# The second block's MLP residual turned by VectorE and sixteen transfers instead of by TensorE

## What is computed

```python
def second_block(x, ...):
    ...
    h = h + y @ w_out[l]
    u = _rmsnorm(h, mlp_norm_g[l])
    h = h + jnp.square(jax.nn.relu(u @ w_up[l])) @ w_down[l]   # the MLP and its residual
    h = _rmsnorm(h, final_norm_g)
    return h[:, N_META:]
```

## Time and profile before

| what | value |
|---|---|
| median of 3 runs | 989.25 us (988.41 to 989.67) |
| the profiled execution | 988.87 us |
| its span in the profile | 987.0 us |
| TensorE busy, of the span | 976.6 us, 99% |
| VectorE, ScalarE, GpSimd busy | 627.5, 470.6, 524.9 us |
| HBM traffic | 110.91 MB read, 2.10 MB written |

### The profile page before, as it was taken

The page is one execution under the profiler, slowest core; times in us unless marked ns, Lnnn a source line. Parts: engine busy times, 40 slices in busy tenths (PEclk is TensorE's granted clock), DMA queues, the critical chain, the costliest instruction groups (busy, mean ns, idle before and its releaser), DMA issues.

```text
span 987.0 us, 12665 instructions
## 1 busy us (share of the span) xinstructions
PE 976.6 (99%) x4827; PEld 827.5 (84%) x4827; DVE 627.5 (64%) x938; ACT 470.6 (48%) x746; POOL 524.9 (53%) x625
## 2 busy tenths in 40 slices
PE   9999999999999999999999999999999999999996
PEld 7888888888888888888899988888888888888885
DVE  5782257665373763274669999874962771595696
ACT  4554445554673223442334866554643443353464
POOL 4555555556555895555656778555056037018212
PEclk9999999999999999999999999999999999999998
DMA  7323221212353225623223123468558347536346
GB/s 238 102 78 126 85 87 44 85 41 68 107 175 124 86 86 134 146 87 127 65 86 107 46 74 118 125 237 193 149 175 197 107 147 185 149 87 182 53 85 171
DMA packets 109116, 117.49 MB, mean 119 GB/s; under 512 B 20434, under 2 KB 86512, under 8 KB 109056
## 3 DMA queue, kind: packets, MB, share of 16 engines
q1 hardware_dynamic: 102304, 102.20, 33.1%
q0 software_dynamic: 6448, 14.16, 8.4%
q10 hardware_dynamic: 304, 0.33, 0.1%
HBM read 110.91 MB, written 2.10 MB: 114 GB/s over the span
## 4 chain that ended last, share of the span: by engine, by line
PE 99%; DVE 0%; ACT 0%; DVEq 0%; issue 0%; ACTq 0%
PE ps L585 70%; PE ps L967 15%; PE ps L604 4%; PE ps L730 1%; PE ps L654 1%; PE ps L751 1%; PE ps L715 1%; PE ps L714 1%; PE ps L845 1%; PE ps L1013 1%; PE ps L792 1%; PE ps L637 0%; PE ps L630 0%; PE ps L941 0%; PE ps L879 0%; DVE X L2472 0%
## 5 line engine op out<-in xcount | busy, mean ns | idle before, releaser
L2523 POOL TENSOR_TENSOR wlo<-raw,whi 128x256 fp32r<-128x256 f32 x496 | 400.4, 860 | 216.6 <-ACT whi L1021 216.5
L585 PE MATMUL ps<-Hh,whi 128*128 128x512 f32 x512 | 201.6, 394 | 0.0
L585 PE MATMUL ps<-Hl,whi 128*128 128x512 f32 x512 | 199.5, 390 | 0.0
L1021 ACT ACTIVATE whi<-raw 128x1024 fp32r<-128x1024 f32 (+1 forms) x126 | 132.2, 1050 | 87.4 <-PE ps L585 51.4
L585 PE MATMUL ps<-Ah,whi 128*128 128x512 f32 (+1 forms) x496 | 164.3, 357 | 0.0
L585 PE MATMUL ps<-Al,whi 128*128 128x512 f32 (+1 forms) x496 | 163.5, 356 | 0.0
L585 PE MATMUL ps<-Hh,wlo 128*128 128x512 f32 x512 | 129.4, 389 | 0.0
L585 PEld LDWEIGHTS ps<-Hh,wlo 128*128 128x128 f32 x512 | 96.1, 188 | 20.0
L585 PEld LDWEIGHTS ps<-Hh,whi 128*128 128x128 f32 x512 | 96.2, 188 | 19.6 <-DVE Hl L1620 0.2
L585 PEld LDWEIGHTS ps<-Hl,whi 128*128 128x128 f32 x512 | 96.2, 188 | 19.2
L585 PE MATMUL ps<-Ah,wlo 128*128 128x512 f32 (+1 forms) x496 | 104.8, 356 | 0.0
(11 more groups left out here) (371 smaller groups left out, 1662.8 us busy)
## 6 DMA issues: line engine op xcount, KB each, us to landing
raw<-in_w_in SPq DMA_DIRECT2D x29, 1024.0 KB, 5.3
raw<-in_w_up SPq DMA_DIRECT2D x16, 1024.0 KB, 5.6
Fm<-in_w_down SPq DMA_DIRECT2D x8, 1024.0 KB, 5.0
w_w<-in_w_down POOLq DMA_DIRECT2D x16, 512.0 KB, 5.7
raw<-in_w_in SPq DMA_DIRECT2D x14, 512.0 KB, 3.8
raw<-in_w_att_out SPq DMA_DIRECT2D x4, 1024.0 KB, 5.2
raw<-in_w_sg_out SPq DMA_DIRECT2D x4, 1024.0 KB, 5.2
raw<-in_w_o SPq DMA_DIRECT2D x4, 1024.0 KB, 5.1
```

What stands on the lines that cost most here:

```text
L585: mm = e.matmul(ps[:, bk, 0:c1 - c0], of(j)[:, k % kk, 128 * g:128 * g + 128], x[:, k, c0:c1], start=(start and n == 0), stop=(stop and n ...
L1021: return e.activation(out, src, ACT.Copy, scale=scale)
L2523: ins = e.tensor_tensor(w_lo(j)[:, *cut], raw_tile(j)[:, *cut], f(w_hi(j))[:, *cut], ALU.subtract)
```

## The change

TensorE's and ScalarE's `residual` go. VectorE gets one instead: after `act(0, 3)` it turns x1 in blocks of 32 x 32, two instructions for each `F3[:, n]`, sixteen in all, from `F3` into `F4f`. A 32 x 32 turn leaves each block on the group of 32 partitions on which it was, so SyncE then issues sixteen transfers from SBUF to SBUF: each takes one of four groups of 32 partitions (c) and one of four token groups (i) and copies it, 32 partitions x 32 pieces x 32 floats, to the 32 partitions on which those tokens belong in `Y`. They stand between the two weight blocks that SyncE loads for part 1. The signal `residual_turned` (wait of the first two casts) becomes `residual_blocks`, and VectorE's wait in `out` goes from `residual_set` to `residual_in` of the last transfer; since `out` in part 0 writes `acc`, which is `F4f`, all of part 0's `out` calls now wait for it.

```diff
+        Y_pieces = F1f.rearrange("p (x c f) -> p x c f", c=4, f=32)
+        turned = F4f.rearrange("p (i x f) -> p i x f", i=4, f=32)
@@ sync_program, part loop
                 load_block(up)
+                if part == 1:
+                    w.wait_ge("residual_blocks", 7)
+                    for c in range(4):
+                        for i in range(4):
+                            e.dma_start(Y_pieces[32 * i:32 * i + 32, :, c], turned[32 * c:32 * c + 32, i]).then_inc(
+                                *b.done("residual_in", (c, i), 16))
                 load_block(up + 1)
@@ tensor_program
-            def residual(n):
-                bk = 7 - n % 2
-                ...
-                for i in range(4):
-                    mm = e.transpose(ps[:, bk, 128 * i:128 * i + 128], F3[:, n, 128 * i:128 * i + 128], ident[:])
-                mm.then_inc(*b.done("residual_turned", n))
@@ down_free
                 if n == P_4:
-                    return "residual_set", 7 - r
+                    return "mlp_mean", 0
@@ scalar_program
-            def residual(n):
-                w.wait_ge("x1_late", 3)
-                w.wait_ge("residual_turned", n)
-                src = ps[:, 7 - n % 2, :].rearrange("p (r t c) -> p r t c", r=2, t=2)
-                copy(Y[:, :, n // 4, :, 128 * (n % 4):128 * (n % 4) + 128], src).then_inc(*b.done("residual_set", n))
@@ vector_program
+            def residual(n):
+                to = F4f.rearrange("p (i r c t m f) -> p r c t i m f", i=4, r=2, c=2, t=2, m=4)
+                of = F3[:, n].rearrange("p (r t i f) -> p r t i f", r=2, t=2, i=4)
+                w.wait_ge("products", (J_UP - 1, 3))
+                for r in range(2):
+                    signal = b.done("residual_blocks", n) if r else step()
+                    e.transpose(to[:, r, n // 4, :, :, n % 4], of[:, r]).then_inc(*signal)
@@ out
                     if n != P12 and part == 0:
+                        w.wait_ge("residual_in", (3, 3))
                         e.tensor_copy(y, bank).then_inc(*signal)
                     else:
-                        w.wait_ge(*(("down_out", (part - 1, n, r)) if part else ("residual_set", 7)))
+                        w.wait_ge(*(("down_out", (part - 1, n, r)) if part else ("residual_in", (3, 3))))
@@ part loop of vector_program
                     if n == 3:
+                        if part == 0:
+                            for m in range(8):
+                                residual(m)
                         x_sums(part, P_7)
```

More of the change, by code:

```diff
@@ L994, in tensor_program @@
                         mlp_sums()
-                    if part == 0 and 3 <= n < 7:
-                        residual(2 * n - 6)
-                        residual(2 * n - 5)
                 for n in range(7 if part < 3 else 6):
@@ L1038, in cast @@
                 elif m in (0, 1):
-                    w.wait_ge("residual_turned", 7)
+                    w.wait_ge("residual_blocks", 7)
                 elif before >= 0:
@@ L1529, in scalar_program @@
                     cast(up_tile(0, n) + 2)
-                if n < 7:
-                    residual(2 * n - 6)
-                    residual(2 * n - 5)
                 for i in {3: (0,), 4: (1, 2), 5: (3,), 6: (4,)}.get(n, ()):
```

## The result

The changed kernel takes 992.20 us, median of 8 runs (990.19 to 993.40); the kernel before 988.88 (988.41 to 989.67, 8 runs). The ratio is 1.0032, with a 95% interval of 1.0022 to 1.0041: slower by 0.3%, where I had forecast 985.6 us. The profiled execution took 992.06 us with a span of 990.2, against 988.87 and 987.0.

What follows compares the result with a forecast made beforehand. TensorE, busy 99% of the span at the 2.4 GHz level, bounds the kernel. Removed transposes give -3.63 us, ScalarE, VectorE and SyncE 0: 989.25 - 3.63 = 985.6 us, range 984.8 to 988.6.

Steps and rivals of the forecast that it cites:

- TensorE -3.63: Between up product 3 and the first down product: removing 32 transposes saves 3.63 us, all on the path.
- The 8.7 us of busy time: Summed durations of the 32 transposes, 272 ns each; they overlap, so the prediction did not take this as their price.
- ScalarE and VectorE 0: Dropped copies are off the path; sixteen turns, 5.4 us, fit in VectorE's 12.89 us of idle time: 0 us.
- the lead of VectorE: VectorE takes product 7 out of PSUM by 692 to 694 instead of 698.41, given as 4.4 to 6.7 us earlier.
- SyncE 0: Loads queued behind the sixteen transfers go out later, second block at about 692; needed some 40 us later: 0 us.
- T: Landing of the last of the sixteen transfers, which VectorE's first `out` awaits: 696 us, range 693 to 699.
- The bound of 701.3: Latest landing of the sixteen transfers before TensorE waits, from the 0.56 us slack at P_6's second weight tile.
- P_6's second low part: Tightest place for TensorE: VectorE made this weight tile's part at 720.96, TensorE used it at 721.52, 0.56 us later.
- The price of waiting: At the first `out`: a landing later than 701.3 makes TensorE wait by just the excess.
- Rival 1: Sixteen transfers land late, delaying the first `out`; at twice the piece time +6.1 us, 995.3 us. Chance 0.13.
- Rival 2: GpSimd, held by its own slowed accumulating transfers, delays up tile 7's low part by 0.8 to 3.8 us. Chance 0.13.

Runs made afterwards that it cites:

- The hold: Changed kernel with SyncE's three w_down loads for part 1 held until the accumulating transfer for P_6's first weight sum landed: 986.73 us, ratio 0.9972; repeated, 986.57 us.
- the pure collision: Kernel without the sixteen transfers, with SyncE's second block and three w_down loads held until the low part of P_5's first weight tile is made: 987.97 us, ratio 0.9989.
- thin neighbours: Changed kernel with three of GpSimd's accumulating transfers that run beside the sixteen cut to 64 of 512 columns: 985.67 us, ratio 0.9966.
- the kernel with the first `out` at 699.78: Changed kernel with SyncE's sixteen transfers ahead of both weight blocks, no loads held back: 991.95 us, ratio 1.0026.
- the filler: Changed kernel with eighteen matmuls of no use, 512 columns each, before P_6 in part 0: 990.79 us, ratio 1.0016.

## Why the prediction was wrong

- **TensorE -3.63.** Right: 3.64 in the trace, 3.83 in the time without transfers. The 8.7 us of busy time would have been the wrong number.
- **ScalarE and VectorE 0.** Right, but for a slip in the text (the lead of VectorE was to be 4.4 to 6.4 us by its own numbers, not 6.7). Sixteen turns took 5.33 us (5.4 forecast) and ended at 677.5 (677.4); `x_sums` ran at 677.48; product 7 was taken out of PSUM at 693.84 (692 to 694 forecast).
- **SyncE 0, the step that failed.** I asked only whether what is queued behind the sixteen transfers is needed late itself. It is. But it moved in time, to 699.8 and later, and there it shares the DMA engines with a transfer that is needed at once. I had SyncE free at about 692 and it was free at 699.7. In the kernel before, these loads were spread over 687.6 to 699 and none of them met P_6's. The hold takes this step away (-5.5 us) and the pure collision makes it by itself (+2.6 us, with a landing of 11.6 us). In the changed kernel it cost so much because T had already used up the slack: 3.7 of the 7.9 us in the table are T's.
- **T, mis-sized.** 696 forecast, range 693 to 699, and 701.87 measured. The piece time was about right (16.5 us with thin neighbours, 17.4 in line 508's rows); the neighbours were counted as two transfers of up to 3 us and were three that added 8. By itself T cost little: with the hold, it was 23.5 to 25.1 us after the first issue and the time 1.2 to 1.4 us above the kernel without transfers in three of four measurements (0.1 below in the fourth). Beside the collision it was no longer free.
- **The bound of 701.3.** It assumed that the order from the first `out` on runs in the same time as before. In that order stands a DMA, P_6's weight sum, which I carried along at its old 5.6 us. With 9.8 the bound is worth nothing: the kernel with the first `out` at 699.78 lost nearly as much (3.0 us against 3.3 by the medians). By its own rule the measured 701.87 would have cost 0.6 us. The order was not full either: in the trace of the kernel before, ScalarE's cast already waited for that transfer (GpSimd's issue, then the cast).

```profile
707.17 1.20 POOL L2564 DMA_DIRECT2D w_w<-in_w_down  x1 [16.43 <-DVE w_more L1620]
```

```profile
712.81 2.01 ACT L1021 ACTIVATE whi<-w_w 128x1024 fp32r<-128x1024 f32 x2 [2.57 <-DMA w_w<-in_w_down]
```

The long wait came at another place than the one named, at `out` of P12 for P_6's banks, and in two traces a shorter one at `out` of P11 for P12's. The place that was named, P_6's second low part, shows in five traces with 0.23 to 0.34 us.
- **The price of waiting.** Counted 1 for 1. The wait of 3.83 us brought 2.52 more at half clock. The Trainium skill (TensorE: Matmul & The Clock Gate, Part 1) describes the same fall to 1.2 GHz after idle time; the granted clock of 0.50 agrees, and the filler got 1.4 us back.
- **Rival 1** named the right sign with another mechanism: late landing by itself, which would have cost 0.6 us here. The late landing was half of what happened. **Rival 2** did not occur, though its landing of 7.4 us for the transfer issued at 677.70 (6.3 before) is there: GpSimd's next issue slipped to 685.35, within its slack. No rival had the loads behind the transfers.

## What to carry to other kernels

When a change makes a queue busy, ask not only when the things behind it are needed, but what they will run beside once they leave in a bunch. Add up all delays on one chain before comparing them with its slack: two that are harmless alone can be a loss together. A wait that holds unurgent loads back until an urgent transfer has landed can be worth more than the work that was saved. And a wait of TensorE is to be priced with the half clock behind it.

## What the runs showed of the hardware

- Copies from SBUF to SBUF in pieces of 128 bytes were hardly faster than loads of x from HBM in such pieces: 2 MB in 16.5 us beside thin neighbours, against 17.4 for line 508, both directly behind a 1 MB block. The Trainium skill (DMA: Bandwidth & Descriptors, "Why small descriptors are slow (HBM only)") has the penalty for HBM alone. Here 4 KB pieces of the same bytes were issued in 14.84 us and 128-byte pieces in 22.16, so the measurement decides against it for this kernel.
- The issuing engine pays: SyncE's 22.16 us for sixteen transfers of 128 KB, up to 3.9 us for one, against 0.37 us for the 1 MB block at 675.62, before which SyncE had issued nothing for 8.5 us.
- An accumulating transfer of 512 KB took 5.6 to 6.3 us to land in the kernel before and 9.8 to 11.6 with 3 to 4 MB issued from SyncE within 5 us of it.
- TensorE's granted clock stayed at 2.4 GHz after waits of 1.41 and 1.74 us and was 1.2 GHz after 2.20 and 3.67 us. Before each it had worked without a gap.
